# Two of the four weight sums of a chunk on GpSimd in place of VectorE, in a two-layer gMLP and attention trunk

## The reference

```
h = RMSNorm(x);  z = h @ W_in
A = gMLP gating,  B = differential attention (both from z)
x = x + RMSNorm(concat(A, B) @ W_out)
h = RMSNorm(x);  gate, up = split(h @ W_gate_up)      # 1024 x (2 x 2816)
x = x + RMSNorm((silu(gate) * up) @ W_down)
```

## Time and profile before

| what | value |
|---|---|
| median of 3 runs | 1104.89 us (1104.8 to 1105.08) |
| the profiled execution: its time | 1104.67 us |
| its span, first to last instruction | 1102.9 us |
| mean granted TensorE clock | 0.998 |
| TensorE busy | 1092.0 us, 99% |
| VectorE busy | 585.0 us, 53% |
| ScalarE busy | 577.4 us, 52% |
| GpSimd busy | 577.1 us, 52% |

### The profile page before, as it was taken

One profiled execution on the slowest core, in us unless ns is written; L12 is line 12 of the kernel. 1 busy time (PEld: TensorE's weight loads), 2 busy tenths in 40 slices (PEclk: granted clock), 3 DMA queues, 4 the chain that ended last, 5 costly groups with the idle time before them and its releaser, 6 DMA issues.

```text
span 1102.9 us, 17390 instructions
## 1 busy us (share of the span) xinstructions
PE 1092.0 (99%) x6763; PEld 964.6 (87%) x6763; DVE 585.0 (53%) x982; ACT 577.4 (52%) x1129; POOL 577.1 (52%) x454
## 2 busy tenths in 40 slices
PE   9999999999999999999999999999999999999998
PEld 6777778999999999888887787789999999998886
DVE  4353535878888886000254445548788888830103
ACT  5656584565555554122356557746555555531212
POOL 3524254666666665544434324645766666655440
PEclk9999999999999999999999999999999999999999
DMA  8323213423333333622243221133333333363212
GB/s 277 133 59 96 67 50 96 153 64 103 103 116 107 91 110 133 217 99 97 76 128 129 77 76 59 61 97 129 95 105 108 116 103 92 115 209 116 96 58 77
DMA packets 144777, 118.33 MB, mean 107 GB/s; under 512 B 3747, under 2 KB 119989, under 8 KB 144694
## 3 DMA queue, kind: packets, MB, share of 16 engines
q1 hardware_dynamic: 144692, 117.20, 33.8%
q10 hardware_dynamic: 2, 0.00, 0.0%
HBM read 110.90 MB, written 6.29 MB: 106 GB/s over the span
## 4 chain that ended last, share of the span: by engine, by line
PE 92%; DVE 3%; POOL 2%; ACT 1%; issue 1%; DMA 1%; SPq 0%; DVEq 0%; ACTq 0%
PE banks L583 28%; PE banks L585 28%; PE banks L584 28%; PE banks L642 2%; PE banks L672 2%; PE banks L592 1%; PE banks L657 1%; POOL w_lo L526 1%; PE banks L686 1%; DMA raw<-in_w_in_dram 1%; POOL xg_lo L533 1%; DVE s_part L1646 0%; DVE banks L1639 0%; ACT swap L1153 0%; PE banks L693 0%
## 5 line engine op out<-in xcount | busy, mean ns | idle before, releaser
L508 POOL TENSOR_TENSOR w_lo<-raw,w_hi 128x512 fp32r<-128x512 f32 x204 | 259.5, 1295 | 303.6 <-ACT w_hi L1026 303.6
L526 POOL TENSOR_TENSOR w_lo<-raw,w_hi 128x512 fp32r<-128x512 f32 x200 | 258.0, 1300 | 140.5 <-ACT w_hi L1088 135.8
L583 PE MATMUL banks<-xg_hi,w_hi 128*128 128x256 f32 (+1 forms) x896 | 279.1, 311 | 3.5 <-ACT m L1321 3.5
L585 PE MATMUL banks<-xg_lo,w_hi 128*128 128x256 f32 (+1 forms) x896 | 275.4, 307 | 0.0
L584 PE MATMUL banks<-xg_hi,w_lo 128*128 128x256 f32 (+1 forms) x896 | 275.1, 307 | 0.0
L1026 ACT ACTIVATE w_hi<-raw 128x1024 fp32r<-128x1024 f32 x102 | 106.9, 1056 | 170.9 <-PE banks L585 155.9
L1088 ACT ACTIVATE w_hi<-raw 128x512 fp32r<-128x512 f32 x200 | 125.2, 630 | 124.0 <-DVE raw L1672 67.0
L583 PEld LDWEIGHTS banks<-xg_hi,w_hi 128*128 128x128 f32 x896 | 172.0, 192 | 14.2 <-ACT m L1321 3.9
L585 PEld LDWEIGHTS banks<-xg_lo,w_hi 128*128 128x128 f32 x896 | 172.0, 192 | 8.1
L584 PEld LDWEIGHTS banks<-xg_hi,w_lo 128*128 128x128 f32 x896 | 172.2, 192 | 6.5
L583 PE MATMUL banks<-w_hi,hid_hi 128*128 128x512 f32 x352 | 137.4, 390 | 0.0
(11 more groups left out here) (160 smaller groups left out, 1797.2 us busy)
## 6 DMA issues: line engine op xcount, KB each, us to landing
raw<-in_w_gate_up_dram SPq DMA_DIRECT2D x88, 512.0 KB, 4.0
raw<-in_w_down_dram SPq DMA_DIRECT2D x44, 512.0 KB, 3.5
raw<-in_w_in_dram SPq DMA_DIRECT2D x40, 512.0 KB, 3.7
raw<-in_w_out_dram SPq DMA_DIRECT2D x16, 512.0 KB, 3.5
x_spill<-x_rows SPq DMA_DIRECT2D x8, 512.0 KB, 5.0
x_rows<-x_spill SPq DMA_DIRECT2D x8, 512.0 KB, 5.1
x_rows<-in_x_dram SPq DMA_DIRECT2D x4, 512.0 KB, 7.2
out_dram<-x_rows SPq DMA_DIRECT2D x8, 256.0 KB, 2.0
```

The lines of the kernel that those rows point to most:

```text
L508: last = tt(lo[:, piece], raw_half(l, c, h)[:, piece], hi[:, piece].bitcast(F32), ALU.subtract)
L526: tt(lo, full, hi.bitcast(F32), ALU.subtract).then_inc(w_ready, 1)
L583: mm(o, stat[0], mov[0], start=first, stop=False)
L585: return mm(o, stat[0], mov[1], start=False, stop=last)
```

## The change

The T1 sum and the T3 sum of each chunk are computed by GpSimd instead of VectorE. T1 is written to `raw` in the place of block B11 (so it waits for B11's low part) instead of to PSUM bank 2; T3 stays in the place of B12. GpSimd does both between the low part of B11 and that of B21, and waits for its own earlier results. A new semaphore `t_pool` counts them; `t_added` counts only T2 and T4. ScalarE's high parts of T1 and T3 wait for `t_pool`. VectorE's low part of T1 and its T2 sum now read T1 from `raw`. The orders of ScalarE's and TensorE's queues stay.

```diff
         def t_place(l, f, i):
+            if i == T1:
+                return block_raw(l, f, 0, 0)
             if i == T3:
                 return block_raw(l, f, 0, 1)
             if i == T4:
                 return block_raw(l, f, 1, 0)
-            return bank[T_BANKS[i]]
+            return bank[T2_BANK]
...
+            def factor_sums(l, f):
+
+                b11, b12, b22 = block_raw(l, f, 0, 0), block_raw(l, f, 0, 1), block_raw(l, f, 1, 1)
+                n = NC * l + C_GU + f
+                pool.wait_ge(raw_landed[n % 2][1], 16 * (n // 2 + 1))
+
+                pool.wait_ge(w_ready, low_upto(l, C_GU + f, LOW_OF[B11]))
+                tt(t_place(l, f, T1), b12, b11, ALU.subtract).then_inc(t_pool, 1)
+                pool.wait_ge(t_pool, t_upto(l, f, 0, 2))
+                tt(t_place(l, f, T3), b22, b12, ALU.subtract).then_inc(t_pool, 1)
...
                 for f in range(F0 + 1, FT):
-                    for i in (B11, B21, T3, T4, B22):
+                    factor_low(l, f, B11)
+                    factor_sums(l, f)
+                    for i in (B21, T3, T4, B22):
                         factor_low(l, f, i)
...
-                    act.wait_ge(t_added, t_upto(l, f, {T1: 0, T3: 1, T2: 3, T4: 3}[i], 4))
+                    if i in (T1, T3):
+                        act.wait_ge(t_pool, t_upto(l, f, int(i == T3), 2))
+                    else:
+                        act.wait_ge(t_added, t_upto(l, f, 1, 2))
...
-                    if later:
-                        t_sum(f + 1, T1)
                     if f > F0:
                         hidden(f - 1)
-                    if later:
-                        t_sum(f + 1, T3)
                     if f > F0:
                         hidden_low(f - 1)
```

More of the change, by code:

```diff
@@ L59, in trunk @@
     SETS = [(0, 4, 5), (1, 6, 7)]
-    T_BANKS = {T1: 2, T2: 3}
+    T2_BANK = 3
     SC_BANKS = [(2, 3), (4, 5)]
@@ L266, in trunk @@
         t_added = sem("t_added")
+        t_pool = sem("t_pool")
         t_ready = sem("t_ready")
@@ L565, in _ @@
                 s_low(l, 1, "S3")
-                for i in (B11, B21, T3, T4):
+                factor_low(l, F0, B11)
+                factor_sums(l, F0)
+                for i in (B21, T3, T4):
                     factor_low(l, F0, i)
@@ L1649, in t_sum @@
                 def t_sum(f, i):
[L1650 to L1654, removed]
+                    b22 = block_raw(l, f, 1, 1)
+                    if i == T2:
                         if f == F0:
@@ L1658, in t_sum @@
                         else:
[L1659 to L1665, removed]
                             dve.wait_ge(t_ready, t_upto(l, f - 1, 1, 2))
@@ L1668, in t_sum @@
                     else:
-                        dve.wait_ge(t_added, t_upto(l, f, 2, 4))
+                        dve.wait_ge(t_added, t_upto(l, f, 0, 2))
                         dve.wait_ge(w_ready, low_upto(l, C_GU + f, LOW_OF[B21]))
@@ L1725, in _ @@
                         s_low(j, name)
-                t_sum(F0, T1)
-                t_sum(F0, T3)
                 hidden(0)
```

## The result

The changed kernel takes 1180.22 us (median of 4, 1179.7 to 1180.84) against 1104.99: 1.068 times the time, 95% interval 1.0666 to 1.0693. The forecast was 1186.

The account below looks back on a forecast made before the run. TensorE's instruction stream was taken as the bound, at 10.08 us a chunk; the helpers' loop would now take 12.13. Loops +34.7 and +36.3 plus starts 2 x 5.2 give +81.4 on 1104.67: 1186, range 1138 to 1201.

Parts of the forecast that it names:

- The bound and the coupling: Chunk stage: TensorE bounds at 10.08 us a chunk; helpers' lateness reaches it through ScalarE's copy `m1`, some 2.05 us each.
- The loop, step by step: GpSimd, ScalarE and VectorE in series, from one B11 low to the next: 12.13 us a chunk, 18 steps a layer.
- The last step: Last of each layer's 18 chunk steps: 0.6 us shorter, with no next B11 high ahead of `m1`.
- The 0.75 that the last copy of before had free: Lateness of the `m1` copy that a chunk forgives, about 0.75 us, subtracted once in each layer.
- The GpSimd self-wait: GpSimd's wait for its own earlier result: 0.12 us, only the one before the T1 sum on the path.
- The start: Stage start in each layer: four sums on late GpSimd ahead of `m1` of F0+1, 5.2 us a layer.
- The sum: Whole kernel: +34.7 and +36.3 for the layers' loops, 2 x 5.2 for starts, +81.4 on 1104.67: 1186.1.
- The near tie: Each chunk: GpSimd's B21 low starts 0.04 us before VectorE's low part of T1, which therefore waits to 5.86.
- the rival: Near tie reversed: VectorE's low part of T1 first, B21 low stretched to 1.74, 10.9 us a chunk, total 1142; 18%.
- No contention that counts: VectorE's two-input reads not lengthened beside GpSimd: 9.8 us a chunk, only the starts cost, 1115; 5%.
- The Trainium skill's rule: VectorE's two-SBUF-input instructions contend with GpSimd's SBUF reads; second issuer blocks for the other's whole duration: total near 1194.
- The clock rival: TensorE's granted clock falls at each new stall; if dips last longer, 13 us a chunk and over, 1215 and above; 6%.

Follow-up runs that it names:

- e4: Changed kernel, but VectorE's low part of T1 and T2 sum read PSUM bank 2 instead of T1 in raw (wrong values): 1110.63 us, ratio 1.005.
- e5: Kernel before, plus two GpSimd instructions a chunk behind B11's low part, writing a spare buffer nobody reads: 1112.41 us, ratio 1.0067.
- e8: Changed kernel with one swap in ScalarE's order, hidden_high(f-1) ahead of T1 high of f+1: 1122.05 us, ratio 1.0154.

## Why the prediction was right

**The bound and the coupling.** Right. TensorE was the bound, and what stalls it now is `m1`. The waits are 36 with 63.3 us, short of the 70 to 80 forecast: two of 3.92 at the starts and 34 of about 1.63, where some 2 had been taken.

**The loop, step by step.** From B11's low part at 334.50 as 0, forecast and measured:

| end of the loop's step | forecast | measured |
|---|---|---|
| T1 high starts | 2.75 | 2.75 |
| `hidden_high` starts | 3.38 | 3.29 |
| B21 low starts | 4.58 | 4.47 |
| low part of T1 ends | 6.41 | 6.31 |
| T3 low ends | 7.56 | 7.46 |
| T2 sum ends | 8.11 | 8.01 |
| T4 sum ends | 8.87 | 8.74 |
| T4 low starts | 9.60 | 9.48 |
| next B11 low | 12.13 | 11.96 |

The mechanism held, and from F0+2 on each order. Sizes were off by little. `hidden_high` starts 0.54 behind T1 high and not 0.63: a queued ScalarE instruction starts 0.09 before the end of the one ahead, which the prediction left out (a like overlap stands in the earlier trace rows, 328.35 to 328.85 for an instruction of 0.60). The T4 sum and the two GpSimd instructions at the end took 0.08 less than forecast (8.01 to 8.74 for the sum, 9.48 to 11.96 for the two). Together it is 0.17 us a chunk, 36 x 0.17 = 6.1 us.

**The last step** was to be 0.6 shorter in each layer, for want of a next B11 high ahead of `m1`. It was not: it took 11.96 like the others. The copy stands behind `silu_11`, and that one waits for VectorE's sums (L1700), not for B11 high:

```profile
465.41 0.42 ACT L1346 ACTIVATE silu_t<-silu_t 128x256 f32<-128x256 f32 x1 [0.83 <-DVE silu_t L1700]
```

This step of the path was wrong in the prediction, for 1.2 us in all. The 0.75 that the last copy of before had free came out as 0.65 behind the last `m1` of layer 1 and 0.68 behind that of layer 0.

**The GpSimd self-wait** was taken at 0.12. It is 0.14 from the end of B11's low part (335.79) to the T1 sum, and 0.08 from the T1 sum to the T3 sum.

**The start** was taken at 5.2 us a layer. From the first low part of B11 of F0 to `m1` of F0+1, both layers took 21.2 us before and take 25.7 now (224.72 to 250.39, and 804.94 to 830.61), 4.5 more. TensorE's wait there is 3.92 in place of 1.77. That the sums themselves do it is shown only in part: e4, without contention, is 5.3 us over the kernel before in both layers together, e5 7.5.

**The sum.** The forecast for the profiled execution was 1186.1, and it took 1180.84, 5.3 less. The loop took 6.1 less and the starts 1.4 less; the last steps 1.2 more and the last copies 0.2 more; and 0.8 more lies ahead of the first chunk F0 (its first low part starts at 224.72 against 223.96), where the change has no work. So the 1180 is near 1186 by small sizes that partly cancel, not by every term.

**The near tie** went as forecast in 36 of the 40 chunks: from F0+2 on, B21's low part starts 0.04 to 0.05 ahead and the low part of T1 takes 1.79 to 1.80. In F0+1 of each layer VectorE comes first, at 243.93 against 244.55 in layer 0, while the T3 sum still runs. There its low part takes 1.21 and B21's is the stretched one, 1.73: the rival's order, beside the forecast one in the same trace. e8 makes that order in each chunk. It gave 1122, not the 1142 of the rival, since GpSimd went from the T3 sum straight to B21's low part, 4.05 behind the start of B11's and not 4.58: the period was 10.33 and not 10.9.

**No contention that counts** was priced at 1115 and had 5%. e4 realises it: 1110.6.

**The Trainium skill's rule** on the shared port ("SBUF — State Buffer", section "Who interferes with whom") holds in who contends: e4's same instructions with one input out of PSUM are not stretched. How much is lost differs, as the trace of before showed: GpSimd lost 0.44 where VectorE's instruction alone takes 0.68 (2.99 for two against 2.55). The forecast by the whole 0.68 was 1194, by the rows 1186, and 1180 was measured.

**The clock rival** did not come. Behind the 3.92 us stalls of the two starts the granted clock fell to 0.50, as it had behind one of 1.77 us before. In the steady stage, where TensorE is busy 16.7 to 18.4 of each 20 us, it stays at 1.00:

```profile
252.00:253.00 1.00, 1.00 (x6) 1.00 (x6) 0.63 (x1) 0.24 (x1) 0.86 (x2) 0.50 0.95 268
```

```profile
340.00:360.00 20.00, 16.74 (x138) 16.34 (x137) 14.73 (x18) 8.62 (x18) 15.22 (x13) 1.00 0.26 74
```

The first window is one of 1 us behind the start's stall in layer 0, the second one of 20 us in steady state. Each row gives its length, the busy time of PE, PEld, VectorE, ScalarE and GpSimd, then granted clock, DMA share and GB/s.

## What to carry to other kernels

Before moving an instruction off an engine that isn't the bound, follow the moved result: where it lies decides what its readers contend with. Here moving the data from PSUM to SBUF cost 53 us, and moving the work 21 on top; with the two blocked reads taken away, data and work together cost 5. Look for the serial loop through the helper queues, not for busy shares: GpSimd was busy 59% and idle over 2 us a chunk in the kernel that it slowed. Which of two instructions waits for the other went by a start 0.04 us earlier, and one swap in a queue's order, which turned it round, gave back 58 of the 75 us.

## What the runs showed of the hardware that was not expected

- VectorE's low part of T1, with two SBUF inputs, was issued while B21's low part ran on GpSimd and T3's stood queued behind. It got in between the two in 36 of 36 cases (1.79 to 1.80 us against 0.68 with one input in a bank), and took only 0.45 us from T3's (1.74 for 1.29). The T2 sum, blocked by T3's low part in the same chunks, ended 0.55 to 0.56 us after it each time.
- TensorE idle for 1.63 us of every 12 kept a granted clock of 1.00 through the stage. One stall of 1.77 us in the kernel before was followed by 3 us at 0.50 in layer 0 and by none in layer 1; 3.92 us in the changed kernel by such a stretch in both layers, and 3.5 us in layer 0 of e4 by none. What tells these cases apart stays open.
- GpSimd's wait on its own result costs 0.08 to 0.14 us, against VectorE's 0.07.
